# Three block products instead of four in a compressed-attention stage, on differences made by VectorE

## What is computed

```python
def compress(x, pe, w1, w2):               # CMP_LEN 32, CMP_STRIDE 16, CMP_HIDDEN 128
    ch = x[:, :nch * CMP_STRIDE].reshape(N, nch, CMP_STRIDE, G, hd)
    hsum = 0
    for r in range(m):                     # m = 2
        proj = jnp.einsum('ncsgd,sdh->ncgh', ch + pe[r][:, None, :], w1[r])
        hsum = hsum + proj[:, r:r + n_cmp]
    return jnp.einsum('ncgh,hd->ncgd', jax.nn.gelu(hsum), w2)
```

## Time and profile before

| what | value |
|---|---|
| median of three runs | 1402.93 us (1400.91 to 1403.13) |
| profiled execution, its own time | 1398.26 us |
| its span | 1396.6 us |
| TensorE busy | 1338.3 us (96%), mean granted clock 0.987 |
| VectorE, ScalarE, GpSimd busy | 508.3, 327.9, 172.1 us |
| chain that ended last | TensorE 92%; of it the pieces' line L1049 8% |
| DMA | 171.16 MB, mean 123 GB/s |
| loads for the samples' attention, KB each | chunk 512, part of dilated keys 1792, page 64, window keys 1024 |
| the nine constants, KB | 544.5, 448, 256, 96, 64, 32, 16.5, 16.4, 12 |

### The profile page before, as it was taken

The page is one execution under the profiler, slowest core; times in us unless marked ns, Lnnn a source line. Parts: engine busy times, 40 slices in busy tenths (PEclk is TensorE's granted clock), DMA queues, the critical chain, the costliest instruction groups (busy, mean ns, idle before and its releaser), DMA issues.

```text
span 1396.6 us, 18882 instructions
## 1 busy us (share of the span) xinstructions
PE 1338.3 (96%) x6928; PEld 1044.0 (75%) x6928; DVE 508.3 (36%) x1177; ACT 327.9 (23%) x663; POOL 172.1 (12%) x380
## 2 busy tenths in 40 slices
PE   7999999999999899789999996999999999999999
PEld 6888656777777656557788884788888888888887
DVE  3776433544444241032122116344454453520000
ACT  4776623344444212012000035210000000000000
POOL 1000000111111522423000100211111111100000
PEclk9999999999999999989999998999999999999999
DMA  5422253222231797977472220122222212222223
GB/s 207 190 87 73 98 204 115 83 80 73 61 97 58 260 334 249 323 257 250 157 278 96 76 64 12 46 76 70 66 76 76 73 63 76 76 76 76 76 77 119
DMA packets 80221, 171.16 MB, mean 123 GB/s; under 512 B 10657, under 2 KB 46434, under 8 KB 79234
## 3 DMA queue, kind: packets, MB, share of 16 engines
q1 hardware_dynamic: 61810, 110.94, 24.2%
q10 hardware_dynamic: 13648, 47.49, 9.2%
q0 software_dynamic: 4672, 11.54, 2.5%
HBM read 160.12 MB, written 9.81 MB: 122 GB/s over the span
## 4 chain that ended last, share of the span: by engine, by line
PE 92%; DVE 2%; ACT 2%; SPq 2%; issue 1%; DMA 1%; ACTq 0%; DVEq 0%
PE ps L2081 47%; PE ps L1049 8%; PE ps L493 8%; PE ps L1509 8%; PE ps L548 3%; PE ps L986 2%; PE ps L972 2%; PE ps L958 2%; SPq L1324 1%; PE ps L475 1%; PE ps L496 1%; PE ps L1556 1%; PE ps L1605 1%; PE ps L533 1%; SPq L1321 1%
## 5 line engine op out<-in xcount | busy, mean ns | idle before, releaser
L2081 PE MATMUL ps<-arena 128*128 128x272 f32 (+2 forms) x2624 | 602.3, 392 | 0.0
L2081 PEld LDWEIGHTS ps<-arena 128*128 128x128 f32 x2624 | 498.6, 190 | 103.1 <-issue 0.5
L493 PE MATMUL ps<-arena 128*128 128x272 f32 x512 | 123.1, 399 | 6.8 <-DVE arena L608 6.8
L1049 PE MATMUL ps<-arena 128*128 128x256 f32 x512 | 120.4, 389 | 3.4 <-DVE arena L1156 3.2
L1509 PE MATMUL ps<-arena 128*128 128x272 f32 x512 | 121.2, 395 | 1.6 <-issue 1.0
L493 PEld LDWEIGHTS ps<-arena 128*128 128x128 f32 x512 | 99.0, 194 | 27.6 <-issue 6.8
L1049 PEld LDWEIGHTS ps<-arena 128*128 128x128 f32 x512 | 95.8, 192 | 30.4 <-issue 14.8
L1509 PEld LDWEIGHTS ps<-arena 128*128 128x128 f32 x512 | 96.2, 190 | 28.3 <-issue 9.4
L2373 DVE TENSOR_TENSOR arena<-ps,arena 128x512 f32<-128x512 f32 x44 | 30.4, 691 | 162.1 <-PE ps L2081 162.1
L2060 ACT ACTIVATE arena<-arena 128x560 f32<-128x560 f32 x22 | 14.8, 671 | 300.5 <-DVE arena L2389 300.5
L2251 DVE TENSOR_TENSOR arena<-arena,ps 128x544 f32<-128x544 f32 x16 | 11.5, 720 | 172.7 <-PE ps L2081 172.7
(11 more groups left out here) (300 smaller groups left out, 1218.5 us busy)
## 6 DMA issues: line engine op xcount, KB each, us to landing
arena<-in_w_close SPq DMA_DIRECT2D x92, 512.0 KB, 3.4
arena<-in_pages_cmp SPq DMA_DIRECT2D x128, 128.0 KB, 2.1
arena<-in_past_va ACTq DMA_DIRECT2D x6, 2048.0 KB, 9.4
arena<-in_past_ka ACTq DMA_DIRECT2D x6, 1792.0 KB, 9.7
arena<-in_w_close ACTq DMA_DIRECT2D x16, 512.0 KB, 4.3
arena<-in_w_proj SPq DMA_DIRECT2D x15, 512.0 KB, 3.3
arena<-in_pages_ks SPq DMA_DIRECT2D x80, 64.0 KB, 3.9
o_z<-arena SPq DMA_DIRECT2D x1, 4352.0 KB, 13.1
```

The source lines that it names most:

```text
L493: last = pe.matmul(ps[:, 2 * (j % 2) + a, 0:HALF], w, h[:, k, a * HALF:(a + 1) * HALF], start=(k == 0), stop=(k == KD - 1))
L1049: last = pe.matmul(parts(kv)[r], w1[:, kv, r, s1, :], x[:, kv, s1], start=(s1 == 0), stop=(s1 == 7))
L2081: last = pe.matmul(ps[:, 2 * p + a, 0:cols.stop - cols.start], ring[:, chunk % CLOSE_RING, w * P:(w + 1) * P], rhs(k)[:, cols], start=(k = ...
```

## The change

Blocks are taken in pairs: E is the even block and O the odd block of a pair, and E' the even block of the next pair. The two windows of a pair are written as

- even window: W0 E + W1 O = (W0 + W1) O + W0 (E - O)
- odd window: W0 O + W1 E' = (W0 + W1) O + W1 (E' - O)

so there are three products of 64 pairs by two heads, 128 columns each, in place of two with 256: BOTH, EVEN and ODD. The pages come from the host with even and odd blocks apart. VectorE makes W0 + W1 once (`weights_of_both`, in step 2, behind a wait for the seven stores) and for each sequence and kv the differences E' - O into a new tile and E - O in place (`differences`, three instructions, at the end of the step before EVEN's). The 48 pieces are handed out at nine in eight steps, from step 4 to step 46; EVEN and ODD share a step once in eight. ScalarE's part reads BOTH alone, and VectorE adds it to EVEN and to ODD in two instructions. The new tiles lie where the constants for `attend_sample` were, so `load_constants` moves behind the last product, ahead of the first gate chunks on SyncE's queue.

```diff
@@ tiles
-    second, inner, bent = at(41048, 2, 2, P), at(41560, 2, 2, P), at(42072, 2, 2, P)
+    second, inner, bent = at(41048, 2, 2, P // 2), at(41560, 2, 2, P), at(42072, 2, 2, P)
+    w_both, x_next = at(43772, 2, 8, P), at(45820, 2, 16, 64)
@@ schedule
-        return min(PIECES, max(0, (t - 4) * 3 // 4))
+        return min(PIECES, max(0, (t - 4) * 9 // 8))
@@ SyncE, attend_prompt
         sp.wait_ge(m.stored, 16 * 7)
-        sp.wait_ge(m.h_scaled, QT + 1)
-        m.load_constants(sp)
         for s in range(2, NSEQ):
-            sp.wait_ge(proj_full, 1 + 2 * (s - 2) + 2)
+            sp.wait_ge(proj_full, products(s - 2, 1))
             load_pages(s)
@@ ScalarE
-            act.activation(second[:, kv], parts(kv)[1], ACT.Identity, bias=m.cmp_bias[:, kv:kv + 1])\
+            act.activation(second[:, kv], part(BOTH), ACT.Identity, bias=m.cmp_bias[:, kv:kv + 1])\
@@ TensorE, piece
+            if product == BOTH:
+                pe.wait_ge(diffs_ready, 1)
+            else:
+                pe.wait_ge(diffs_ready, 1 + 2 * s + kv + 1)
+            x = page_view(s, kv).rearrange("p w (e s) n i -> p w s e n i", e=2)
+            follows = x_next[:, kv].rearrange("p (e s) i -> p s e i", e=2)
             for s1 in range(8):
-                last = pe.matmul(parts(kv)[r], w1[:, kv, r, s1, :], x[:, kv, s1], start=(s1 == 0), stop=(s1 == 7))
-            if r == 1:
+                w, rhs, out = {BOTH: (w_both[:, kv, s1, :], x[:, 1, s1], part(BOTH)),
+                               EVEN: (w1[:, kv, 0, s1, :], x[:, 0, s1], part(EVEN)),
+                               ODD: (w1[:, kv, 1, s1, :], follows[:, s1, :, 0:63], part(ODD)[:, :, 0:63])}[product]
+                last = pe.matmul(out, w, rhs, start=(s1 == 0), stop=(s1 == 7))
+            if product == ODD:
                 last.then_inc(proj_full, 1)
@@ VectorE
-            dve.tensor_tensor(hid[:, s % 2, kv, :, 0:NCMP_S], second[:, kv, :, 1:P], parts(kv)[0][:, :, 0:NCMP_S],
+            dve.wait_ge(proj_full, products(s, kv))
+            window = hid[:, s % 2, kv].rearrange("p e (i w) -> p w e i", w=2)
+            dve.tensor_tensor(window[:, 0], part(EVEN), second[:, kv], ALU.add)
+            dve.tensor_tensor(window[:, 1, :, 0:63], part(ODD)[:, :, 0:63], second[:, kv, :, 0:63],
                               ALU.add).then_inc(proj_free, 1)
+
+        def weights_of_both():
+            dve.wait_ge(w_in, 16 * 4)
+            dve.wait_ge(m.stored, 16 * 7)
+            dve.wait_ge(m.h_scaled, QT + 1)
+            dve.tensor_tensor(w_both[:, :, :, :], w1[:, :, 0], w1[:, :, 1], ALU.add).then_inc(diffs_ready, 1)
+
+        def differences(s, kv):
+            x = page_view(s, kv)
+            dve.wait_ge(page_in[s % 2], 16 * NPAGE * (s // 2 + 1))
+            if s >= 1:
+                dve.wait_ge(proj_full, products(s - 1, kv))
+            after = x_next[:, kv].rearrange("p a (n i) -> p a n i", i=4)
+            step.done(dve.tensor_tensor(after[:, :, :, 0:3], x[:, 0, :, :, 1:4], x[:, 1, :, :, 0:3], ALU.subtract))
+            step.done(dve.tensor_tensor(after[:, :, 0:NPAGE - 1, 3], x[:, 0, :, 1:NPAGE, 0],
+                                        x[:, 1, :, 0:NPAGE - 1, 3], ALU.subtract))
+            step.wait()
+            dve.tensor_tensor(x[:, 0], x[:, 0], x[:, 1], ALU.subtract).then_inc(diffs_ready, 1)
@@ VectorE's loop
+            if t == P_PROJ + 1:
+                weights_of_both()
...
+            for s in range(NSEQ):
+                for kv in range(2):
+                    if step_of(s, kv, EVEN) - 1 == t:
+                        differences(s, kv)
@@ SyncE, attend_sample
-        sp.wait_ge(m.proj_full, 1 + 2 * NSEQ)
+        sp.wait_ge(m.proj_full, m.products(NSEQ - 1, 1))
+        m.load_constants(sp)
         for c in range(CLOSE_RING):
             m.load_chunk(sp, c)
```

More of the change, by code:

```diff
@@ L728, in width, with step_of, products @@
         return (units[i][2] + 1) * P
-    PIECES = NSEQ * 4
+    BOTH, EVEN, ODD = range(3)
+    PIECES = NSEQ * 6
     def pieces_before(t):
-        return min(PIECES, max(0, (t - 4) * 3 // 4))
-    def step_of(piece):
+        return min(PIECES, max(0, (t - 4) * 9 // 8))
+    def step_of(s, kv, product):
+        piece = 6 * s + 3 * kv + product
         return next(t for t in range(STEPS) if pieces_before(t + 1) > piece)
     def seq_step(s):
-        return step_of(4 * s + 3)
+        return step_of(s, 1, ODD)
+    def products(s, kv):
+        return 1 + 2 * s + kv + 1
     assert pieces_before(STEPS) == PIECES
@@ L778, in queries_of, with part, page_view @@
         return QA + j if kind == DIL else QB + j
-    def parts(kv):
-        v = ps[:, PROJ, :].rearrange("p (r g c) -> p r g c", r=2, g=2)
-        return v[:, 0], v[:, 1]
+    def part(product):
+        return ps[:, PROJ, P * product:P * product + P].rearrange("p (g i) -> p g i", g=2)
+    def page_view(s, kv):
+        return pages[:, s % 2].rearrange("p n (v a w i) -> p v w a n i", v=2, a=16, w=2)[:, kv]
     def p_parts(kv):
@@ L789, in grouped @@
         return v.rearrange("p (g c) -> p g c", g=2)
+    m.products = products
     m.s_uses, m.s_dve_uses = len(s_users), sum(not k for k in by_act)
@@ L898, in second_half @@
         def second_half(s, kv):
[L899 to L900 removed]
+            act.wait_ge(proj_full, products(s, kv))
+            act.activation(second[:, kv], part(BOTH), ACT.Identity, bias=m.cmp_bias[:, kv:kv + 1])\
                 .then_inc(second_ready, 1)
@@ L929, in on_act @@
                 for kv in range(2):
-                    if step_of(4 * s + 2 * kv + 1) + 1 == t:
+                    if step_of(s, kv, ODD) + 1 == t:
                         bend(s, kv)
@@ L940, in on_act @@
                 for kv in range(2):
-                    if step_of(4 * s + 2 * kv + 1) == t:
+                    if step_of(s, kv, ODD) == t:
                         second_half(s, kv)
@@ L1040, in piece @@
         def piece(n):
[L1042 to L1045, removed]
+            s, kv, product = n // 6, n // 3 % 2, n % 3
+            if product == BOTH:
+                if kv == 0:
+                    pe.wait_ge(page_in[s % 2], 16 * NPAGE * (s // 2 + 1))
                 pe.wait_ge(proj_free, 2 + 2 * s + kv)
-            x = pages[:, s % 2].rearrange("p n (v e s c) -> p v s e n c", v=2, e=2, s=8)
-            for s1 in range(8):
-                last = pe.matmul(parts(kv)[r], w1[:, kv, r, s1, :], x[:, kv, s1], start=(s1 == 0), stop=(s1 == 7))
-            if r == 1:
+            if product == BOTH:
+                pe.wait_ge(diffs_ready, 1)
[3 more added lines that the diff above has]
+            follows = x_next[:, kv].rearrange("p (e s) i -> p s e i", e=2)
+            for s1 in range(8):
+                w, rhs, out = {BOTH: (w_both[:, kv, s1, :], x[:, 1, s1], part(BOTH)),
[3 more added lines that the diff above has]
+            if product == ODD:
                 last.then_inc(proj_full, 1)
@@ L1342, in on_sync @@
         SP = mybir.EngineType.SP
-        sp.wait_ge(m.proj_full, 1 + 2 * (NSEQ - 2) + 2)
+        sp.wait_ge(m.proj_full, m.products(NSEQ - 2, 1))
         for i in range(2):
@@ L1400, in on_pool @@
             if g == 0:
-                pool.wait_ge(m.proj_full, 1 + 2 * NSEQ)
+                pool.wait_ge(m.proj_full, m.products(NSEQ - 1, 1))
                 for i in range(2, 4):
```

6 lines of the change are left out of this document (3 added, 3 removed).

## The result

The changed kernel took 1410.09 us (1404.9 to 1415.27) beside 1402.93 for the kernel before, each the median of 11 runs: ratio 1.0050, 95% interval 1.0033 to 1.0068. It is slower by half a per cent, 7.2 us, where 1404.3 was forecast with a range of 1395 to 1412. Its profiled execution took 1412.52 us for a span of 1410.8. The 4.7 us of before go with the clock: in the rounds of the experiments its executions with a mean granted clock of 0.987 or 0.988, as in this profile, took 1395.0 to 1399.1 us, those with 0.981 to 0.985 took 1399.3 to 1404.6.

A forecast was written before the change was run, and what follows sets the result against it. The prompt's attention was taken as bound by TensorE's issue. Gain until step 41, delay from the moved constants and the clock's fall summed as -6.9 + 5.4 + 2.9 = +1.4 us, taking 1402.93 to 1404.3, range 1395 to 1412.

The forecast's parts named there:

- rival 5: VectorE becomes the stage's bound, differences of 3.1 us ahead of EVEN costing 7.1 us: 1411.4 us, chance 0.21.
- The product: TensorE's products of 128 columns, 16 records each: 1.80 us a product, with 1.75 and 2.0 as ends.
- Rival 7: TensorE's weight loads don't overlap with columns in this shape: 3.57 us a product, 1475 us, chance 0.02.
- The differences: VectorE's three differences per sequence and key or value, 768, 240 and 1024 elements: 2.46 us.
- The waits before EVEN: TensorE waits for VectorE's differences: 1.5 to 1.8 us behind 512 keys, 0.3 behind 128, none where EVEN and ODD share.
- the walk: Eight attention steps followed through VectorE's and TensorE's order: 39.4 us against 40.6, about 1.2 to 1.3 us gained.
- The beginning: Attention's start up to step 12, including VectorE's sum of the weights: 2.2 us saved, ends 0 and 4.
- Rival 6: VectorE waits at step 2 for the stores, all units behind it: some 4 us, 1408 us, chance 0.06.
- The constants: Nine loads moved on SyncE's queue make page scores wait: 5.4 us lost, plus 2.9 us from the clock's fall.
- Rival 3: SyncE catches up on its 16 pages, up to 5.4 us come back: 1396.0 us, chance 0.14.
- Rival 4: The walk's waits don't appear in the stage, if differences are ready one step earlier: 1394.9 us, chance 0.07.
- Rival 2: Same as the forecast without the clock's fall, as the wait splits over gates, keys and pages: 1401.4 us, chance 0.15.

The follow-up runs named there:

- late: Kernel before, with only the nine constants' loads moved behind the last product, ahead of the gate chunks: 1413.02 us, ratio 1.0080.
- late_tiny: Kernel before, nine constants moved likewise, each cut to 16 rows and all but one to 16 columns: 1410.62 us, ratio 1.0073.
- vw: Changed kernel, with GpSimd's window values of group 0 issued only behind the scores of SyncE's pages: 1407.53 us, ratio 1.0045.
- order: Changed kernel, with SyncE's 16 pages issued ahead of the second part of the dilated keys: 1409.75 us, ratio 1.0047.
- ahead: Changed kernel, with VectorE's whole differences placed one step earlier, two steps ahead of EVEN: 1393.49 us, ratio 0.9951.
- bare: Changed kernel, with VectorE's differences nearly left out, a few elements kept, places and signals unchanged: 1387.97 us, ratio 0.9895.

## Why the prediction was right and wrong

The sign was open in the forecast (slower had 0.38; the items that it names add to 0.41), and the time fell into the range, whose upper part rival 5 had put there. The likeliest case, no change that can be told, didn't come, and both large terms were off to the same side.

**The product: right.** 1.80 us was forecast; 1.84 to 1.89 were measured. Rival 7 is refuted: 16 loads and 16 matmuls of 128 columns in 1.84 us are 0.115 us a pair, where the earlier trace rows had 0.113 for a load with fewer columns beside it. One sentence of the Trainium skill ("TensorE: Matmul & The Clock Gate", Part 3 on packing small matmuls) lets a load overlap a running matmul only in other rows of the array; the trace disagrees with it, these take all 128 rows. The same section also names loads into a background weight buffer, and with that the trace agrees.

**The differences: 2.46 forecast, 2.73 measured.** The 768 and the 1024 elements took 0.95 and 1.23, as reckoned; runs of 3 and 4 elements cost nothing. The miss is the small one, 240 elements in 0.60 us, mean 599 ns over the stage, where 0.40 was taken. Its inputs are single numbers 1 KB apart. The Trainium skill ("SBUF — State Buffer", the section on the DMA port swizzle, its note on lines of 16 bytes) says that each access to a new line of 16 bytes pays; this row agrees, but no run here varied the stride.

**The waits before EVEN: the place right, the price wrong.** Forecast: 1.5 to 1.8 us once in eight steps, 0.3 behind a unit of 128 keys, nothing at the step of EVEN and ODD. Measured: 1.9 to 2.1, 0.7 to 1.0, and 0.7 in three of four cases. That is the 0.27 that VectorE was longer, in three places, as rival 5 put it, and some 0.3 more. What the walk had no term for is the clock: it charged low clock only behind the 7.8 us wait at the end, and the shortest wait that it showed with a fall behind it was 3.06 us. In the changed stage waits of 1.88 to 2.14 us were enough in 14 of 24 cases, and a fall cost 1.0 to 1.7 us. In eight steps:

| us | forecast | after |
|---|---|---|
| waits for the differences | 2.1 | 3.4 |
| waits from ODD to BOTH | 1.7 | 0.8 |
| low clock | 0 | 1.0 |
| work | 35.6 | 35.7 |
| eight steps (terms rounded) | 39.4 | 41.0 |

**The step that failed is this one: from 1.2 us gained in eight steps to 0.4 lost in this trace, 0.1 gained in those with fewer falls.** The gain to unit 44 was then 1.5 us (beyond the 0.8 that the span started earlier), not 6.9; in the five other traces of the same stage unit 44 came up to 3.4 us earlier still.

**The beginning: 2.2 forecast, 3.2 measured** up to unit 12, with the sum of the weights at 2.28 us right behind the weights of unit 1, at 233.47. Rival 6 falls: it waited for nothing.

**The constants: 8.3 forecast, about 11 measured** (late), for partly wrong reasons. Right were the place, the length of the issue (5.7 us) and the clock's fall. The interval of late reaches down to 8.4, so by time alone the sum is hardly refuted. It took 5.4 us for the delay, the mean of 5.0 by bytes and 5.8 by issue, but late_tiny has hardly any bytes and costs the same within its interval. What the traces show beside it is that during the issue the DMA engines are partly idle (a busy share of 0.65 in after, 0.10 in late_tiny, where before has 0.94 at this place), just ahead of some 20 us in which they are full. It is argued from these traces, and not shown by a run of its own, that whatever isn't moved in the gap pushes the last pages back, and that then other queues' loads, released by TensorE's progress and not by SyncE's, come in beside the late pages (1 MB of window values at 487.60, against 491.37 before, and ScalarE's chunk at 482.65). The pages do end later by more than they start later. How much of the extra 7.6 us of issue is due to each of these wasn't split; vw shows 3.9 for the window values in one profile, order 7.0 for the second keys, and the two overlap.

**Rival 3** (SyncE catches up) expected the reverse of what happened. **Rival 4** (no waits in the stage, 1394.9) named its own condition, differences ready one step earlier; ahead is that kernel, at 1393.49, though its own time is reached with different terms (a larger gain in the stage, a larger loss behind it). **Rival 5** has its place and its mechanism confirmed by ahead and bare. Its time, 1411.4, is nearest to the result, but by luck: it needs 3.1 us of differences, and the 2.73 measured give 3 x 0.27 x 29 / 8 = 2.9 us by its own rule, 1407.2; the clock, which it doesn't name, made up more. By the ratios only about half of the 5.8 us between forecast and result lies in the stage (4 us gained, not 6.9) and half behind it (11 lost, not 8.3). Rival 2 falls with the clock.

The edits that remove both causes give 1386.5 us, 1.05% under the kernel before: the three products do pay, once VectorE has their differences ready and the loads at the end are put in another order.

## What to carry to other kernels

When work moves from the bound engine to another one, reckon its latency at the place where it is put, not its share of an idle engine, and price a wait with the clock that it can cost: one step earlier was worth 14 us with not an instruction less. Moving small loads in a queue can cost as much without their bytes as with them, if what stands behind them feeds DMA engines that are about to be full. Try the bulk loads first and the small ones behind them (here with two more edits it gave 8 us), and look at which other queues will start beside what is now late. Where the clock falls in one execution and not in the next, read several traces of the same stage before putting a number on it.

## What the runs showed of the hardware

Behind the same four waits in six traces of the same stage TensorE's granted clock fell to 1.2 GHz five times at 1.88 us, three times at 2.08, five times at 2.14 and once at 1.91, and stayed at 2.4 GHz the other ten times; a wait of 3.06 us near the stage's end stands in all thirteen traces, and behind it six transposes took 1.20 to 1.51 us in seven (1.21 in before) and 0.84 or 0.85 in six (0.85 in after). No run explains which. One issue among the nine constants, a load of 64 KB in 128 rows of 512 bytes, took 2.0 to 4.1 us on SyncE's queue in every kernel that issued it whole (2.17 in before), and 8.5 and 11.7 on ScalarE's; the others, 12 to 544.5 KB, took 0.3 to 1.5; cut to 16 rows with the loads ahead of it, it took 0.42. In after, from 470 to 495 us, the 16 DMA engines at a share of 0.90 to 1.04 moved 309 to 398 GB/s of pages, keys and chunks.
